# A decoder trunk on eight cores: the depthwise convolution as banded matrices over four token phases, ordered first transfers, and longer weight rings

## What is computed

```python
def conformer_conv_mixer(h, w_in, b_in, dw, dw_b, ln_g, ln_b, w_out, b_out):
    """Pointwise+GLU -> causal depthwise conv (width 31) -> channel LayerNorm -> swish -> pointwise."""
    D = h.shape[-1]
    a, gate = jnp.split(h @ w_in + b_in, 2, axis=-1)
    u = a * jax.nn.sigmoid(gate)                         # GLU, (B,S,D)
    u = lax.conv_general_dilated(
        u, dw.astype(u.dtype)[:, None, :], window_strides=(1,),
        padding=[(CONV_WIDTH - 1, 0)],                   # left padding only: causal
        dimension_numbers=('NWC', 'WIO', 'NWC'), feature_group_count=D) + dw_b
    u = jax.nn.silu(layer_norm(u, ln_g, ln_b))
    return u @ w_out + b_out
```

## Time and profile before

| | us |
|---|---|
| runs of the kernel before: median, lowest, highest | 6425.09, 6423.67, 7243.81 |
| profiled execution: its own time | 6432.7 |
| profiled execution: span of the slowest core (core 5) | 6431.2 |
| spans of the eight cores | 6413.7 to 6431.2 |
| mean granted TensorE clock of the cores | 0.974 to 0.977 |

### The profile page before, as it was taken

How to read it: one execution, slowest core, us unless ns; L and a number is a source line. 1 busy time by engine, 2 the same in 40 slices (tenths; PEclk the granted TensorE clock), 3 DMA queues, 4 the chain that set the end, 5 groups by cost and what they waited for, 6 DMA issues and landing times.

```text
span 6431.2 us, 87780 instructions; the slowest of 8 cores (6413.7 to 6431.2 us)
## 1 busy us (share of the span) xinstructions
PE 5992.4 (93%) x31128; PEld 2833.2 (44%) x31128; DVE 3361.0 (52%) x4215; ACT 2073.5 (32%) x3101; POOL 1016.0 (16%) x791
## 2 busy tenths in 40 slices
PE   4999988999999997899989999889999999878999
PEld 2444543444444433444444455434444444333444
DVE  2445566544544497553454455564444444866445
ACT  3116883211312222321151188732131131233213
POOL 1002440000000453000000034200000005420000
PEclk9999999999999998999999999999999999989999
DMA  6222313322320301222352223223232221031322
GB/s 109 40 40 26 32 22 50 45 40 40 47 40 14 42 1 27 37 40 40 63 128 40 35 31 32 44 38 47 38 42 34 40 29 20 1 55 21 43 37 63
DMA packets 368262, 258.52 MB, mean 40 GB/s; under 512 B 114625, under 2 KB 331713, under 8 KB 367840
## 3 DMA queue, kind: packets, MB, share of 16 engines
q0 software_dynamic: 348288, 211.84, 24.8%
q1 hardware_dynamic: 19552, 41.06, 2.1%
HBM read 441.61 MB, written 16.78 MB: 71 GB/s over the span
## 4 chain that ended last, share of the span: by engine, by line
PE 85%; DVE 5%; issue 4%; ACT 2%; DMA 1%; POOL 1%; SPq 1%; DVEq 0%; ACTq 0%; POOLq 0%
PE ps L635 38%; PE ps L650 19%; PE ps L893 5%; PE ps L742 3%; PE ps L839 3%; PE ps L972 3%; PE ps L729 3%; PE ps L857 2%; PE ps L1061 2%; PE ps L559 2%; PE ps L993 1%; DVE arena L765 1%; SPq L503 1%; PE ps L755 1%; DMA arena<-xattn_wkv 1%
## 5 line engine op out<-in xcount | busy, mean ns | idle before, releaser
L635 PE MATMUL ps<-arena 128*128 128x512 bf16 x11264 | 2491.8, 381 | 16.4 <-DVE arena L765 10.5
L635 PEld LDWEIGHTS ps<-arena 128*128 128x128 bf16 x11264 | 1101.6, 98 | 1338.8 <-issue 41.7
L638 DVE TENSOR_TENSOR arena<-ps,arena 128x512 bf16<-128x512 f32 x704 | 486.1, 691 | 1765.5 <-PE ps L635 1757.5
L637 ACT ACTIVATE arena<-ps 128x512 bf16<-128x512 f32 x704 | 420.0, 597 | 2728.5 <-PE ps L635 2724.9
L650 PE MATMUL ps<-arena 128*128 128x512 bf16 x5632 | 1248.9, 379 | 0.5 <-DVE h L652 0.3
L652 DVE SCALAR_TENSOR_TENSOR h<-ps,h 128x512 f32<-128x512 f32 x1536 | 1040.9, 689 | 218.5 <-PE ps L650 212.7
L650 PEld LDWEIGHTS ps<-arena 128*128 128x128 bf16 x5632 | 550.7, 98 | 662.3 <-issue 2.0
L586 POOL DMA_DIRECT2D arena<-ffn_w_in x176 | 154.6, 880 | 2613.0 <-PE ps L635 2118.7
L893 PE MATMUL ps<-arena 128*128 128x512 bf16 x1984 | 461.9, 392 | 41.7 <-DVE arena L869 29.1
L531 ACT ACTIVATE junk<-h 128x1024 bf16<-128x1024 f32 x288 | 303.7, 1054 | 314.6 <-DVE h L589 182.6
L972 PE MATMUL ps<-arena 128*128 128x512 bf16 x1536 | 382.1, 387 | 0.0
(11 more groups left out here) (143 smaller groups left out, 4679.5 us busy)
## 6 DMA issues: line engine op xcount, KB each, us to landing
arena<-ffn_w_in POOLq DMA_DIRECT2D x176, 512.0 KB, 7.9
arena<-ffn_w_out POOLq DMA_DIRECT2D x88, 512.0 KB, 6.8
arena<-hgrn_w_in POOLq DMA_DIRECT2D x64, 256.0 KB, 5.3
arena<-xattn_wkv POOLq DMA_DIRECT2D x16, 1024.0 KB, 13.0
y<-arena SPq DMA_DIRECT2D x32, 512.0 KB, 2.9
h<-x SPq DMA_DIRECT2D x20, 512.0 KB, 5.7
arena<-xattn_wq POOLq DMA_DIRECT2D x8, 1024.0 KB, 8.7
arena<-xattn_wo POOLq DMA_DIRECT2D x8, 1024.0 KB, 9.3
```

Source lines behind the costliest of these rows:

```text
L635: P.op("pe", lambda e, bb=bb, ga=ga, k=k, j=j: e.matmul(psb(bb), lhsT=wiv[:, ga, k, j * 128:(j + 1) * 128], rhs=hnT[:, k, blk * 512:(blk + ...
L637: P.op("act", lambda e, bg=bg, j=j: e.activation(out=sg[j].ap, in_=psb(bg), func=AF.Silu), reads=psk(bg), writes=sg[j].keys())
L638: P.op("dve", lambda e, bu=bu, j=j, q=q: e.tensor_tensor(out=actv[:, q, :], in0=psb(bu), in1=sg[j].ap, op=ALU.mult), reads=psk(bu) + sg[j] ...
```

## The change

The convolution stage is written anew, and three smaller things go with it.

**Convolution.** Tokens are split into four phases (`q`, token index modulo 4), channels into 32 groups of 32 (`gi`). `glu` writes one chunk of 128 channels with its tokens sorted by phase (`uT`, one chunk only). `relayout` is 16 DMAs on SP's queue, each 32 partitions by 512 tokens, from `uT` to `U`: there the partitions hold 4 phases x 32 channels of one group. `conv` then needs 9 matmuls for each group and block of tokens: stationary is a window of `U` (128 positions of 4 tokens), moving a banded 128x128 matrix (L872, POOL, one for each group, two buffers) that holds the 31 taps for every pair of phases. The result has tokens on partitions and 32 channels of the 4 phases in 128 columns; DVE adds `dw_b` and writes it into `U2`, float32, all tokens and channels. `relayout` of the next chunk writes each (`g`, `q`) piece of `U` after the matmuls of that group have read it. The layer norm now works along the free axis: sums by ACT with an accumulator (`stats`, 768 channels after chunk 5, 256 after chunk 7), the four numbers of a block in `moments`, then for phases 0 and 1 two DVE operations, for 2 and 3 one on ACT and two on POOL, a SiLU into the single buffer `y` (L947), eight transposes (L950), a DVE copy to channels on partitions (L951), and the 64 output matmuls of the block (L957). `hook(b)` is called after each block.

**First transfers.** Token tiles 4 to 7 are issued when the halves of the first weight group have landed, tile `tt` from 8 on when `tt - 4` has, and the other first weights behind tiles 11 to 15. The vectors and the taps wait for an ACT operation (`tick`) that reads `h[0]` in pack 2; the model of time now gives a vector load 10 us more.

**Rings.** `wi` and `wo` get 5 slots each, and the next FFN goes on at the slot after the last one used.

```diff
-        self._set(60.0, 2000.0 + n * 4 / 230.0)
+        self._set(60.0, 2000.0 + n * 4 / 230.0 + (10000.0 if allow_slow_non_contiguous else 0.0))
...
+        dwS = sb("dwS", [128, D // 32, 36], BF16)
+        mask32 = sb("mask32", [128, 32], BF16)
+        lst = sb("lst", [128, 6, 16], F32)
...
+            P.op("sp", lambda e: e.dma_start(out=vecs[:, slot, :], in_=src.rearrange("(c p) -> p c", p=128), allow_slow_non_contiguous=True), reads=["tick"], writes=[("vec", slot)], dma=True)
...
+            for q in range(4):
+                P.op("pool", lambda e, q=q: e.dma_start(out=dwrep[:, :, q, :], in_=cv_dw_d[0].rearrange("j (g c) -> j g c", c=32)), reads=["tick"] + (["dwr0"] if q else []), writes=(["dwr0"] if not q else []) + [("dwr", q)] + (dwrep_buf.keys() if not q else []), dma=True)
...
-            NW, NO, NA = 3, 4, 3
+            NW, NO, NA = 5, 5, 3
...
+            base = ring[0]
...
+                s = (base + g) % NW
...
+                lead(wi[base % NW].keys(0, KC * 256), wi[base % NW].keys(KC * 256, 2 * KC * 256), lambda: load_wo(0, [("landed", 0, 5)]))
...
+                load_wo(0)
+            for g in range(1, NW):
+                late = () if lead is None else [("landed", 0, (11, 13, 15, 15)[g - 1])]
+                load_wi(g, late)
+                if g < NO:
+                    load_wo(g, late)
...
-                    for g in pack:
-                        if g + 2 < NG:
-                            load_wo(g + 2)
+                    for g in (packs[packs.index(pack) - 1]):
+                        if NO <= g + NO < NG:
+                            load_wo(g + NO)
...
-            uT = CV.take(KC * TP, BF16)
...
+            U2 = CV.take(NB * 4 * D, F32)
...
+            wi = [CV.take(KC * 256, BF16) for _ in range(2)]
...
+            uT = CV.take(T, BF16)
+            U = CV.take(4 * (NQ + PADQ), BF16)
+            bd = [CV.take(36 * 32, BF16) for _ in range(2)]
...
+            gn = (gslot[0] - 1) % 2
+            ga = gslot[0] % 2
             gslot[0] += 1
-            load_gain(g, cv_bout_d[0])
+            load_gain(gn, cv_bout_d[0])
+            load_gain(ga, cv_dwb_d[0])
...
+            def glu(c):
+                v = wi[c % 2].ap.rearrange("p (a k n) -> p a k n", a=2, n=128)
+                for blk in range(NB):
+                    bg = P.bank()
+                    ba = P.bank()
+                    for (bb, a) in ((bg, 1), (ba, 0)):
+                        for k in range(KC):
...
+                    P.op("act", lambda e, bg=bg, s=s, c=c: e.activation(out=sg[s].ap, in_=psb(bg), func=AF.Sigmoid, bias=vecs[:, V_BG, c:c + 1]), reads=psk(bg) + [("vec", V_BG)], writes=sg[s].keys())
+                    P.op("dve", lambda e, ba=ba, s=s, c=c, blk=blk: e.scalar_tensor_tensor(out=uTv[:, :, blk * 128:(blk + 1) * 128].rearrange("p q t -> p t q"), in0=psb(ba).rearrange("p (t q) -> p t q", q=4), scalar=vecs[:, V_BA, c:c + 1], in1=sg[s].ap.rearrange("p (t q) -> p t q", q=4), op0=ALU.add, op1=ALU.mult),
...
+            def relayout():
+                for g in range(4):
+                    for q in range(4):
+                        P.op("sp", lambda e, g=g, q=q: e.dma_start(out=Uv[32 * q:32 * q + 32, g, PADQ:PADQ + NQ], in_=uTv[32 * g:32 * g + 32, q, :]), reads=uT.keys() + [("uT", blk) for blk in range(NB)], writes=[("U", g, q)], dma=True)
...
+            def build_band(gi):
...
+                P.op("pool", lambda e: e.tensor_tensor(out=v, in0=mask32[:, None, :].to_broadcast([128, 36, 32]), in1=dwS[:, gi, :, None].to_broadcast([128, 36, 32]), op=ALU.mult),
...
+            def conv(c):
+                for g in range(4):
+                    gi = 4 * c + g
+                    s = gi % 2
+                    v = bd[s].ap
+                    b = P.bank()
+                    for blk in range(NB):
+                        for d in range(9):
+                            P.op("pe", lambda e, b=b, blk=blk, d=d, g=g, v=v: e.matmul(ps[:, P.place[b], blk * 128:(blk + 1) * 128], lhsT=Uv[:, g, blk * 128 + d:blk * 128 + d + 128], rhs=v[:, d * 128:(d + 1) * 128], start=(d == 0), stop=(d == 8)),
+                                 reads=bd[s].keys() + U.keys() + Uk(g), writes=psk(b))
+                    P.op("dve", lambda e, b=b, gi=gi: e.tensor_tensor(out=U2.ap.rearrange("p (a c) -> p a c", c=D)[:, :, gi * 32:(gi + 1) * 32], in0=psb(b).rearrange("p (a c) -> p a c", c=32), in1=gB[:, ga, None, gi * 32:(gi + 1) * 32].to_broadcast([128, 16, 32]), op=ALU.add),
+                         reads=psk(b) + [("gB", ga)], writes=[k for a in range(16) for k in U2.keys(a * D + gi * 32, a * D + (gi + 1) * 32)])
+                    if gi + 2 < NG32:
+                        build_band(gi + 2)
...
+            def stats(b, part):
+                lo, hi = ((0, 768), (768, D))[part]
...
+            for gi in range(2):
+                build_band(gi)
+            glu(0)
+            relayout()
+            for c in range(KC):
+                if c + 1 < KC:
+                    glu(c + 1)
+                    for tt in range(c * 16 // 7, (c + 1) * 16 // 7):
+                        bout_add(tt)
+                conv(c)
+                if c + 1 < KC:
+                    relayout()
+                if c == 5:
+                    for b in range(NB):
+                        stats(b, 0)
             for hf in range(2):
...
+            for b in range(NB):
+                stats(b, 1)
+                moments(b)
+                slot = (3, 2, 3, None)[b]
+                if slot is None:
...
+                for q in (2, 0, 3, 1):
+                    a = b * 4 + q
...
+                    if q < 2:
+                        P.op("dve", lambda e, b=b, q=q, a=a: e.scalar_tensor_tensor(out=u2v[:, b, q, :], in0=u2v[:, b, q, :], scalar=lst[:, 0, a:a + 1], in1=gB[:, ga, :], op0=ALU.subtract, op1=ALU.mult), reads=uk + [("lmean", b), ("gB", ga)], writes=uk)
+                        P.op("dve", lambda e, b=b, q=q, a=a: e.scalar_tensor_tensor(out=u2v[:, b, q, :], in0=u2v[:, b, q, :], scalar=lst[:, 5, a:a + 1], in1=lnb.ap, op0=ALU.mult, op1=ALU.add), reads=uk + lnb.keys() + [("lrs", b)], writes=uk)
+                    else:
+                        P.op("act", lambda e, b=b, q=q, a=a: e.activation(out=u2v[:, b, q, :], in_=u2v[:, b, q, :], func=AF.Identity, scale=lst[:, 5, a:a + 1], bias=lst[:, 1, a:a + 1]), reads=uk + [("lrs", b), ("lnm", b)], writes=uk)
+                        P.op("pool", lambda e, b=b, q=q: e.tensor_tensor(out=u2v[:, b, q, :], in0=u2v[:, b, q, :], in1=gB[:, ga, :], op=ALU.mult), reads=uk + [("gB", ga)], writes=uk)
+                        P.op("pool", lambda e, b=b, q=q: e.tensor_tensor(out=u2v[:, b, q, :], in0=u2v[:, b, q, :], in1=lnb.ap, op=ALU.add), reads=uk + lnb.keys(), writes=uk)
+                    P.op("act", lambda e, b=b, q=q: e.activation(out=y.ap, in_=u2v[:, b, q, :], func=AF.Silu), reads=uk, writes=y.keys())
+                    bt = P.bank()
...
+                        P.op("pe", lambda e, c=c, bt=bt: e.transpose(out=psb16(bt)[:, c * 128:(c + 1) * 128], in_=y.ap[:, c * 128:(c + 1) * 128], identity=ident[:]), reads=y.keys() + ["ident"], writes=psk(bt))
+                    P.op("dve", lambda e, bt=bt, q=q, yTv=yTv: e.tensor_copy(out=yTv.rearrange("p c (t r) -> p c t r", r=4)[:, :, :, 3 - q], in_=psb16(bt).rearrange("p (c t) -> p c t", t=128)), reads=psk(bt), writes=yk)
...
+                hook(b)
...
+                P.op("act", lambda e: e.activation(out=stat[0:1, 0, 31:32], in_=stat[0:1, 0, 0:1], func=AF.Copy), reads=[("ss", 0), ("h", 0)], writes=["tick"])
...
-                def lead(g0=g0):
-                    for blk in range(1, NB):
+                def lead(k0, k1, then, g0=g0):
+                    for tt in range(4, 8):
+                        load_x_tile(0, tt, "pool", k0 if tt < 6 else k1)
+                    norm_block(1, g0)
+                    then()
+                    for blk in range(2, NB):
                         for tt in range(blk * 4, blk * 4 + 4):
-                            load_x_tile(0, tt, "pool")
+                            load_x_tile(0, tt, "pool", [("landed", 0, tt - 4)])
                         norm_block(blk, g0)
```

249 lines of the change are left out of this document (94 added, 155 removed).

## The result

The changed kernel takes 0.9686 of the time before (95% interval 0.9647 to 0.9726): 3.1% faster, where 6.1% was forecast. In some executions, whatever the kernel, the cores of a die show a lower granted clock and take longer; these are left out here, and the others of the changed kernel took 6214 to 6235 us. The profiled one took 6235.0, span 6233.5, against 6041 in the prediction's sum: 194 us more.

The account below looks back on a forecast made before the run. PE's work was taken as the bound (93% busy). From the profiled 6432.7 us, minus 320 for both convolution stages, minus 75 for the start, plus 3 for tap transposes, gave 6041; against the median 6033, forecast 6030, range 5950 to 6160.

Parts of the forecast that it names:

- the start's gain of 75: Start of the kernel: ordered first transfers cut PE's loss from 103 to 27 us; gain 75, bounds 45 and 90.
- the rival that made the kernel slower: Convolution stage: relayout transfers set the pace; slower than before from 3 us a transfer, 7024 us at 5.7; chance 0.04.
- The two signs that the prediction named as proof of error: Convolution stage: L883's releaser a DMA, or the tail's L950 released by ACT for over 80 us in a sequence.
- DVE: four products as L845, 0.75 each: GLU chunks: DVE's four products at 0.75 us and four adds of like size make 6 us, keeping up with PE.
- T: The last banded product, end of the convolution proper; forecast 189 us into the stage.
- DVE has some 19 us of work for each block: End of the stage: DVE's passes, four copies, adds and hook take some 19 us, under a block's 26.
- The tail, T + 132: End of the stage: from last banded product to last output product 132 us, bounds 105 to 165.
- the seam of 4 us: Start of the convolution stage: the first relayout waits behind the gain reload and POOL's bias adds, costing 4 us.
- half clock: Rival, end of the stage: output products and transposes run at half clock, +126 us, 6155; 0.22 together with longer tail.
- longer ACT chain: Rival, end of the stage: a SiLU stands behind a waiting Square, 30 us a sequence, 6090; 0.22 together with low clock.
- The vectors and taps now come in pack 2, where weights are three groups ahead.: Start: no wait for taps expected; the 32 small tap transposes cost 3 us once.
- Deeper rings gain nothing; they cost nothing: FFN weight rings: products never waited for weights after the start, so deeper rings change the time by nothing.

Follow-up runs that it names:

- e3: Changed kernel with the GLU product written to neighbouring elements and read with a step of four: 0.9620 of the time before.
- c1: Changed kernel with taps in one transfer, bias adds held back and GLU product written in a row: 0.9537 of the time before.
- e4: Changed kernel with the copy of transposed y written in a row, result rows left in another order (timing only): 0.9625 of the time before.
- e5: Changed kernel with the 24 small sums of blocks 1 to 3 held until the block before has its four SiLUs: 0.9693 of the time before.
- c4: c1 plus rebuilt end (y in place, four-phase row-written copies), small sums held for block 0 only, DVE normalising all tiles: 142 us ahead of changed kernel, core 0.
- c5: Changed kernel with all repairs: c4's edits plus weight rings starting at slot 0 behind attention: 0.9433 of the time before, spans 6033 to 6055 us.
- e2: Changed kernel with POOL's 16 bias adds held back until the second chunk and later: 0.9606 of the time before.
- e1: Changed kernel with taps loaded in one contiguous transfer and laid out four times by DVE copies: 0.9635 of the time before.
- e8: Changed kernel with the weight rings at their old depth of 3 and 4 and old output-weight request point: run ends 3 us later, core 2.
- e10: Changed kernel with the FFN behind attention starting its weight rings at slot 0 again: 0.9632 of the time before.

## Why the prediction was wrong, by its own steps

**What held.** That PE's work is the bound; 70 us of banded products (69); the bands at 2.1 to 2.4 (2.17); the start's gain of 75 from the ordered first transfers (72.4), with the first product at 20 us; PE's busy time near 5650 (5689). The relayout was not the pace, and the rival that made the kernel slower fell with it: PE waited 7.1 us for it in all. The two signs that the prediction named as proof of error did not come: L883's main releaser was DVE, not a DMA, and ACT held the tail's L950 for 23.6 us, not 80. It was wrong without them. The DMA issues of the changed kernel:

```profile
arena<-arena SPq DMA_DIRECT2D x256, 32.0 KB, 1.8
```

One lands in 1.8 us, and they are issued 0.6 us apart, so they overlap. The banded products took 60 ns each (138.7 us over 2304). The Trainium skill ("TensorE: Matmul & The Clock Gate", Back-to-back issue gap) has 81 ns for such a pair, and the trace does not agree.

**What failed.** Of the 194 us, 101 were lost in the two convolution stages, 25 in the FFNs before them, 20 at the lower clock, 19 at the taps, 17 behind the stages, 9 in between and 3 at the start. The steps of the prediction that failed:

1. The step "DVE: four products as L845, 0.75 each". I took the form (512 columns, the same operands) and passed over the pattern of the write, which the diff shows. It is 2.6 us. e3 prices it at 23 us in all; with the taps and the bias adds mended as well (c1), T comes at 197 and 195, 6 to 8 us over the 189. The same slip stands in the tail, where the copy of `y` was put among "DVE has some 19 us of work for each block": 2.45 a copy, 11 to 15 us a sequence by e4.
2. The tail, T + 132, came out at 158, the seam of 4 us at 12, and T at 214 for 189. The tail's steps had the right chain (ACT's sums, then a block at a time) but POOL's passes counted once, at 4.7 us; two tiles stand behind one another, 9.3, and DVE is slowed meanwhile. The rivals "half clock" and "longer ACT chain", 0.22 together, had this direction. The first had a small part: the four blocks of output products lasted 15.2, 15.5, 17.4 and 13.7 us against 13.8 each, 7 us more, of which the sum held 2.6. The granted clock stood at half for 75 of these 158 us, but PE was busy in only 22 of the 75. The second had part of the cause: e5 took 9 us off the first wait, and shows that ACT's queue alone is not the cure. That c4 and c5 end at T + 129, in a stage of 324 and 320 us, suggests that the 132 was a fair sum for the work, not for these writes and this sharing (the two kernels also order the end of the stage differently).
3. The bias adds. I used them only for what stands behind them on SP's queue, and named POOL and DVE as separate engines. They ran beside the hooks' scaling and cost 12 us a sequence in the FFN and 8 more in the stage, where the last two hooks lie (e2). The Trainium skill ("SBUF — State Buffer", SBUF: two separate sides) says that GpSimd holds a port pair which DVE needs for operations with two operands in SBUF, and that the loser waits for the whole instruction. The trace agrees: DVE took 9.05 us against 4.87, and the bias adds themselves up to 3.3 us each where in e2 they take 2.36. I had not weighed it.
4. "The vectors and taps now come in pack 2, where weights are three groups ahead." I priced the transposes at 3 us and the load at nothing; it is four transfers in a row of 21 us each, and PE stood 20.5 us (e1: 23).
5. "Deeper rings gain nothing; they cost nothing". The depth gave nothing in steady FFNs, as said; behind the badly loaded taps it was worth 16 us (e8). The rotation of the first slot, which I read in the diff and did not cost, moved the order behind attention: 14 to 16 us a sequence (e10).
6. The clock and the core. The time is that of the slowest core, and the range had no term for one core losing time by itself. This core ran its last 120 us at 0.81, which cost 20 us, below; in the execution of 6214 us no core's mean clock is under 0.965. And the stage of 483.1 us that both sequences were counted from was the longest of its trace; the mean of the cores was 474.

With steps 1 to 5 undone, c5 is 172 us ahead of the changed kernel on core 0 (part of it, the y in place and no POOL, is more than the change had promised), and step 6 is another 20 of the 194. The range failed because its bounds were around sums of work: the tail of 158 even lay inside its own bound of 165, while T was bounded by the bands alone, and the taps, the FFN before and the order behind had no bound at all. No single rival was the case: five losses of 15 to 50 us came together.

## What to carry to other kernels

Take a duration from a row only if the access pattern matches too, writes above all: here a step in a bf16 write made the same DVE instruction 3.5 times as long, and swapping the order of its walk so that the step falls on the read took all of it back. When work leaves PE, ask of each operation that it hands to POOL which DVE operation runs beside it, and of each small rearranging transfer how many stand in a row on its queue. With a planner, look at the order it makes near every stage whose buffers move, and tell it the true prices.
